# A decoder layer on one core: the first output panel of each MLP group in two passes over the contraction, and another order of ScalarE's copies and squares

## What is computed

```python
h2 = _rmsnorm(x, g_ffn)
x = x + jnp.square(jax.nn.relu(h2 @ w_ff1)) @ w_ff2
gate = jax.nn.sigmoid(_rmsnorm(x, g_ple) @ w_ple_gate)
x = x + gate * (pe @ w_ple_proj)
```

## Time and profile before

| | us |
|---|---|
| median of 3 runs | 1080.73 |
| lowest, highest | 1079.89, 1082.28 |
| the profiled execution's own time | 1075.9 |
| its span, first to last instruction | 1074.1 |
| TensorE matmul busy in it | 1032.9 (96%) |
| VectorE, ScalarE busy | 759.2 (71%), 551.3 (51%) |

### The profile page before, as it was taken

How to read it: one execution, slowest core, us unless ns; L and a number is a source line. 1 busy time by engine, 2 the same in 40 slices (tenths; PEclk the granted TensorE clock), 3 DMA queues, 4 the chain that set the end, 5 groups by cost and what they waited for, 6 DMA issues and landing times.

```text
span 1074.1 us, 20914 instructions
## 1 busy us (share of the span) xinstructions
PE 1032.9 (96%) x8340; PEld 1015.7 (95%) x8340; DVE 759.2 (71%) x973; ACT 551.3 (51%) x1305; POOL 243.0 (23%) x374
## 2 busy tenths in 40 slices
PE   8999999999998999999999998999999999989996
PEld 8999999999988998999999998999999999989996
DVE  5579888988887778989573377448637744855552
ACT  6772888569635554352264475316613731663331
POOL 2441334014220023949101210001001000102300
PEclk9999999999998999999999999999999999999998
DMA  6557555776698565867742336536644653653512
GB/s 200 195 177 229 195 189 183 256 227 213 213 273 257 161 197 153 217 192 210 241 134 80 99 128 221 190 127 221 229 166 165 229 192 127 221 189 130 164 40 84
DMA packets 131104, 196.41 MB, mean 183 GB/s; under 512 B 32208, under 2 KB 108272, under 8 KB 129216
## 3 DMA queue, kind: packets, MB, share of 16 engines
q1 hardware_dynamic: 105808, 122.46, 35.7%
q0 software_dynamic: 10304, 63.28, 17.7%
q10 hardware_dynamic: 14896, 9.34, 2.9%
HBM read 186.07 MB, written 62.00 MB: 231 GB/s over the span
## 4 chain that ended last, share of the span: by engine, by line
PE 78%; DVE 7%; ACT 5%; issue 3%; DMA 3%; SPq 2%; ACTq 1%; POOL 0%; DVEq 0%
PE gm L1296 32%; PE gm L1539 6%; PE gm L1272 6%; PE gm L1273 5%; PE gm L1274 5%; PE psSO L1296 5%; PE psSO L1539 4%; PE psT L1539 3%; PE psT L1296 3%; PE gm L1280 1%; PE gm L1281 1%; PE psSO L1476 1%; PE psSO L1451 1%; ACT prob L1089 1%; DVE w_lo L1626 1%
## 5 line engine op out<-in xcount | busy, mean ns | idle before, releaser
L1272 PE MATMUL gm<-w_hi,h_hi 128*128 128x256 f32 x640 | 187.3, 293 | 3.7 <-issue 3.5
L1273 PE MATMUL gm<-w_hi,h_lo 128*128 128x256 f32 x640 | 181.1, 283 | 0.0
L1274 PE MATMUL gm<-w_lo,h_hi 128*128 128x256 f32 x640 | 180.4, 282 | 0.0
L1296 PE MATMUL gm<-h_hi,w_hi 128*128 128x272 f32 x640 | 135.2, 292 | 0.3 <-issue 0.3
L1296 PE MATMUL gm<-h_hi,w_lo 128*128 128x272 f32 x640 | 132.4, 288 | 0.0
L1296 PE MATMUL gm<-h_lo,w_hi 128*128 128x272 f32 x640 | 132.0, 288 | 0.0
L1272 PEld LDWEIGHTS gm<-w_hi,h_hi 128*128 128x128 f32 x640 | 121.2, 189 | 6.2 <-issue 4.8
L1274 PEld LDWEIGHTS gm<-w_lo,h_hi 128*128 128x128 f32 x640 | 121.6, 190 | 0.0
L1273 PEld LDWEIGHTS gm<-w_hi,h_lo 128*128 128x128 f32 x640 | 121.0, 189 | 0.0
L2225 POOL DMA_DIRECT2D out_kvs<-in_cache_kv_w x64 | 34.9, 546 | 368.1 <-PE gm L1296 120.8
L1619 DVE TENSOR_TENSOR w_lo<-w_raw,w_hi 128x1024 fp32r<-128x1024 f32 x80 | 95.5, 1232 | 29.4 <-ACT w_hi L735 28.9
(11 more groups left out here) (343 smaller groups left out, 2650.3 us busy)
## 6 DMA issues: line engine op xcount, KB each, us to landing
out_kvs<-in_cache_kv_w POOLq DMA_DIRECT2D x64, 510.0 KB, 4.8
w_raw<-in_w_in SPq DMA_DIRECT2D x60, 512.0 KB, 6.4
w_raw<-in_w_ff SPq DMA_DIRECT2D x38, 512.0 KB, 5.8
kv<-in_cache_kv_w SPq DMA_DIRECT2D x128, 128.0 KB
kv<-in_cache_kv_w SPq DMA_DIRECT2D x64, 256.0 KB
out_kvs<-in_cache_kv_w POOLq DMA_DIRECT2D x32, 508.0 KB, 5.2
w_more<-in_w_ff SPq DMA_DIRECT2D x26, 512.0 KB, 6.8
kv<-in_cache_kv_w POOLq DMA_DIRECT2D x128, 64.0 KB, 3.4
```

Source lines behind the costliest of these rows:

```text
L1272: nc.tensor.matmul(out, lh, wh, start=k == 0, stop=False)
L1273: nc.tensor.matmul(out, ll, wh, start=False, stop=False)
L1274: last = nc.tensor.matmul(out, lh, wl, start=False, stop=k == KD - 1)
L1296: last = nc.tensor.matmul(pair[:, half, 0:HALF], w, x[:, k0 + k, half * HALF:(half + 1) * HALF], start=first, stop=end)
```

## The change

Four edits. (1) TensorE makes the first output panel of each group in two passes: contraction blocks 0 to 5 of both units, then blocks 6 and 7 of both (`early_and_late`). (2) In seven-product panels ScalarE's `part(p,1)` and `part(p,2)` are put ahead of `squares_hi(p-1,..)`; in the first such panel `raw_hi(p+1,1)` goes between the two. (3) In the last group panel q = 5 is loaded to `w_more` and no more to `w_raw`, and ScalarE's first `gained_hi(1,0)`, which overwrites it, waits until it is split. (4) In the panels before a seven-product one, `sums_hi(p+1,1,1)` and `pair_lo(p+1,1,1)` go ahead of the second hidden unit.

```diff
-    if p < ff_panel(0, 3) or p >= P_PG or j == NFF - 1 and q > 4:
+    if p < ff_panel(0, 3) or p >= P_PG or j == NFF - 1 and q > 5:
...
                 act.wait_ge(z_used, zu)
+                if n == 1 and m == 0:
+                    act.wait_ge(w_lo_done, SPLITS[ff_panel(NFF - 1, 5)] + 2)
...
                 if new:
                     part(p, 0)
-                if after:
+                if p != SEVENS[0] and (after or not new):
                     raw_hi(p + 1, 1)
-                elif not new:
-                    raw_hi(p + 1, 1)
+                if new:
+                    part(p, 1)
+                    if p == SEVENS[0]:
+                        raw_hi(p + 1, 1)
+                    part(p, 2)
                 if seven(p - 1):
                     squares_hi(p - 1, 0)
                     squares_hi(p - 1, 1)
                 if new:
-                    part(p, 1)
-                    part(p, 2)
                     if not after:
                         raw_hi(p + 1, 1)
...
+                    if after and sub:
+                        sums_hi(p + 1, 1, 1)
                     if q < 4:
                         hidden_unit(j, 2 * q + sub)
...
-                if after:
-                    sums_hi(p + 1, 1, 1)
...
+            def early_and_late(p, early):
+
+                j, u = (p - P_FF) // FF_PANELS, U_FF + 2 * (p - P_FF)
+                r = weights_in(p)
+                for k0, k1 in ((0, early), (early, KD)):
+                    for sub in range(2):
+                        if k0 == 0:
+                            pair_free(u + sub)
+                        for k in range(k0, k1):
+                            if sub == 0:
+                                pe.wait_ge(hid_lo, j * KD + (k + 1))
+                            wh, wl = [x[:, r, k * 256 + 128 * sub:k * 256 + 128 * sub + 128] for x in (w_hi, w_lo)]
+                            for w, x, first, end in ((wh, x2_hi, k == 0, False), (wh, x2_lo, False, False), (wl, x2_hi, False, k == KD - 1)):
+                                for half in range(2):
+                                    last = nc.tensor.matmul(banks(u + sub)[:, half, 0:HALF], w, x[:, k, half * HALF:(half + 1) * HALF],
+                                                            start=first, stop=end, skip_group_check=True)
+                        if k1 == KD:
+                            last.then_inc(unit_ready, 1)
...
+                if q == 4:
+                    early_and_late(p, 6)
+                    return
...
-                        wk = (lambda k: (hid_lo, j * KD + (k + 1))) if uu == 8 else None
-                        block_unit(r, 256, 128 * sub, KD, banks(u), x2_hi, x2_lo, 0, wk)
+                        block_unit(r, 256, 128 * sub, KD, banks(u), x2_hi, x2_lo)
...
+                    if after and sub:
+                        pair_lo(p + 1, 1, 1)
...
-                if after:
-                    pair_lo(p + 1, 1, 1)
```

## The result

The changed kernel is a little slower: median 1082.32 us (20 runs, 1079.80 to 1087.61) against 1079.81 us of the kernel before (20 runs beside it, 1077.76 to 1085.49), ratio 1.0026, 95% interval 1.0013 to 1.0038. That is +2.8 us, between +1.4 and +4.1. Forecast were +4.5 us and slower by over 0.2%; the interval's lower end lies under that bound.

A forecast was written before the change was run, and what follows sets the result against it. TensorE, busy 96% of the span, bounds the kernel, so only its standstills and halved clock matter. -14.4 + 14.7 + 1.25 = +1.5 us, plus 3 for clock drops, gives +4.5: 1080.73 to 1085.2 us, range 1081 to 1089.

The forecast's parts named there:

- What is taken away: In q4, two passes and the other buffer remove the waits for `x_lo`: gain up to 14.4 us.
- The ring of late squares: In q1 to q4, squares queued behind copies make weights late: net 4.9 us per group 1 to 3, 1.25 in group 0.
- casts of sums later by: ScalarE's casts of sums in q1 of group 1 come 3.07 us later than before, and all behind them too.
- gap ahead of q4, with the restart: TensorE stands ahead of q4 until the late cast of its weights is split: 2.3 us with the restart.
- q1 start to q4 start, group 1, over before: Net loss of a group from q1 to q4: 1.6 + 1.6 + 2.3 = 5.5, 0.6 back, 4.9 us.
- The rival that the squares pass the copies: ScalarE's queue lets ready squares pass waiting copies, nothing late: -16 us, 1064.7; within the faster rival, chance 0.16.
- the rival that lateness is absorbed: In q2 and q3 late weights are mostly absorbed, only q4's late cast costs: -8.05 us, 1072.7; faster rival, chance 0.16.
- The drops of the clock after the change: Behind the four gaps ahead of q4, two clock drops of 1.25 to 1.5 us each: +3; bounds 0 to +6.
- the clock before the change: In q4 before, clock drops after waits counted within the 14.4 us excess; waits had lowered it in one group of three.
- the 14.4 us of excess: q4 of groups 0 to 3 over an undisturbed 12.03 us panel: 2.35 + 2.35 + 3.85 + 5.85 us.
- the 4.8 us between that execution and the median: Whole kernel: profiled execution of before is 4.8 us under the median of runs; difference carried to the forecast median.
- at full clock: Sum over the whole kernel before pricing new clock drops: -14.4 + 14.7 + 1.25 = +1.5 us.

The follow-up runs named there:

- the filled kernel: Kernel before, with matmuls on constant operands put into the two waits of q4's first unit: 1074.23 us (8 runs), ratio 0.9945.
- its filled form: Constant-operand matmuls put into the kernel before's q4 waits: 1074.23 us, ratio 0.9945; or 16 put ahead of each q4 in the changed kernel: 1079.55 us, ratio 0.9991.
- the first experiment: Changed kernel with only ScalarE's order of copies and squares put back as before: 1062.04 us, ratio 0.9820 to the kernel before.
- the miss with p7: Changed kernel with `part(p,2)` moved behind both units' squares, `part(p,1)` left ahead: 1070.31 us, ratio 0.9911 to the kernel before.

## Why the prediction was nearly right

**What is taken away.** Right. The waits for `x_lo` are gone, q4 takes 12.1 us at full clock, and the passes and the buffer without the new order give -1.8%. By the medians that is 18.2 us, where the rows gave 14.4. The stretch gives 15.6: 14.4 of it from q4, the rest from the shorter q1 and q2 that came with edit 4. What the medians have over the stretch is answered below.

**The ring of late squares.** Right in mechanism and in every term:

| term, us | forecast | profile after |
|---|---|---|
| squares of q1 begin, into the panel | 6.5 | 6.53 |
| casts of sums later by | 3.07 | 3.08 |
| q2 | 12.17 | 12.20 |
| gap ahead of q4, with the restart | 2.3 | 2.21 (14.41 - 12.20) |
| q1 start to q4 start, group 1, over before | 4.9 | 4.91 |

The Trainium skill's rule, ScalarE's and VectorE's queues strictly first in, first out (TensorE: Matmul & The Clock Gate, section on the array of 16 sub-arrays), agrees with these rows: the relu of q1 ran at 743.02, directly behind a copy that had waited 1.13 us. The rival that the squares pass the copies, and the rival that lateness is absorbed, fall with q2 and q3.

**The drops of the clock after the change.** Two drops, 1.5 us each, forecast +3; by the ratios 3.8 us. That it was two is in part luck: the rows only bounded it between none and four, and the forecast took the middle.

**The step that failed in size: the clock before the change.** The forecast took the 14.4 us of excess, drops of the earlier trace rows with it, as what q4 loses in any execution, and carried the 4.8 us between that execution and the median over to the sum unchanged. But its drops are a draw: two of four groups, worth 3.3 us by the panels of the filled kernel, where a like kernel (the buffer alone) drew three, and where filling the same waits is worth 5.9 us at the median. So the change takes away more clock than the profiled execution had shown. With each part at its measured size:

| term, us | forecast | measured |
|---|---|---|
| at full clock | 1.5 + 3.3 = +4.8 | 0.9991 - 0.9945 = 0.46%, +5.0 |
| clock, after | +3.0 | +3.8 |
| clock, before (taken away) | -3.3 | -5.9 |
| sum | +4.5 | +2.9 |

The measured sum is the measured 1.0026 by construction; what the experiments add is its split. The intervals are wide (2.6 us to either side for the last term), so that the whole of the difference lies in the last line is the likeliest reading and is not shown to a microsecond.

The mean clocks of all the executions give the two clock terms a second time. The lower of TensorE's two levels is half of the upper, so (1 - mean clock) x span / 0.5 is the time at the lower one. It averages, to about 1 us each, 28.0 us in the 19 executions of before that ran beside its filled form and 16.6 in that form, 25.3 in the changed kernel and 17.6 in its filled form. Where TensorE sets the pace, half of such a difference is lost: 5.7 us and 3.8 us, beside the 5.9 and 3.8 of the table.

This also corrects what can be said of before's profiled execution. It was not fast for want of time at the lower level in all, of which it had 28.5 us; only two of its drops lay in q4. And of the 3.9 us that it is under its median, a part lies ahead of the stretch, where the kernels hardly differ: its q2 of group 0 began at 648.82 us, that of the other ten profiled executions at 648.96 to 654.58, in the middle 650.9. So carrying the whole difference between one execution and the median over to the sum was right for that part and wrong for the clock in q4. It answers for the first experiment too: its stretch is 15.6 us under before's, its median 18.2 us, and the 2.6 us between them are about what the median of before loses in q4 beyond its profile (5.9 - 3.3).

**What stays open.** Why gaps of the same 2.06 us bring the clock down in one group and not in another was not settled.

## What to carry over

A copy may go ahead of other work in a queue only once the product it copies is due, or the ready work waits for that product; here the two copies cost 2.1% ahead of two units' squares, and nothing that the intervals show with one between the units and the other behind both. After such a move follow both chains through one whole turn of the loop, that of the work now behind and that of the moved piece's own reader, as the miss with p7 shows. Where idle time can bring the clock down, one profile shows one draw, and its distance from the median need not be the clock's: price the drops of the kernel before as carefully as those of the changed one, and measure them by filling the gaps.

## What was unexpected in the hardware

Gaps in an otherwise busy TensorE cost more than their length, and unevenly. Four gaps of 2.06 us brought two drops; pairs of 0.6 and 1.2 us, 1.8 us in all, one drop in three groups in the profile before and three in four in the kernel with the buffer alone, of 1.5 us each. Filling them with matmuls whose results are not used took the drops away and was worth 0.35% of the run in the changed kernel and 0.55% in the one before, with the same work waiting for the same inputs.
